# Split rows for the first two experts, and gate products put ahead of down products, in a mixture-of-experts encoder layer

## The reference, cut to what matters

```python
h = layer_norm(x) * (1 + scale2) + shift2
g = argmax over 4 groups; two best of that group's 8 experts     # hierarchical router
for each chosen expert e of a token:                               # SwiGLU, 1024 -> 512 -> 1024
    y_e = (silu(h @ w_exp_gate[e]) * (h @ w_exp_up[e])) @ w_exp_down[e]
f = sum over the two experts of weight * y_e
x = layer_norm(alpha * x + gate2 * f) * ln2_g + ln2_b
```

## Time and profile before

| | |
|---|---|
| median of 3 runs | 959.95 us (956.57 to 960.58) |
| the profiled execution | 959.74 us |
| its span, first to last instruction | 958.1 us |
| mean granted TensorE clock | 0.982 |
| PE busy | 908.5 us, 95% |
| DVE, ACT, POOL busy | 375.9, 244.6, 113.6 us |
| DMA | 295.53 MB, mean 308 GB/s |

### The profile page before, as it was taken

How to read it: one execution, slowest core, us unless ns; L and a number is a source line. 1 busy time by engine, 2 the same in 40 slices (tenths; PEclk the granted TensorE clock), 3 DMA queues, 4 the chain that set the end, 5 groups by cost and what they waited for, 6 DMA issues and landing times.

```text
span 958.1 us, 11740 instructions
## 1 busy us (share of the span) xinstructions
PE 908.5 (95%) x4381; PEld 547.7 (57%) x4381; DVE 375.9 (39%) x646; ACT 244.6 (26%) x357; POOL 113.6 (12%) x142
## 2 busy tenths in 40 slices
PE   3999999999999999999999999999998999998994
PEld 2567766888888888786454444444444444443331
DVE  4533443565344236798531232222221231322135
ACT  2422244432333225446411111101011110111024
POOL 2210366000001000000000000000000000000031
PEclk9999999999999999999999999999998999999997
DMA  9985654265565623809999999999999999999974
GB/s 370 348 282 175 253 218 177 89 230 208 200 240 147 183 91 114 278 0 401 384 404 400 410 427 425 427 424 429 429 426 424 375 395 427 426 426 427 423 290 136
DMA packets 47510, 295.53 MB, mean 308 GB/s; under 512 B 5046, under 2 KB 7190, under 8 KB 32082
## 3 DMA queue, kind: packets, MB, share of 16 engines
q1 hardware_dynamic: 37216, 263.99, 68.6%
q0 software_dynamic: 9616, 29.02, 9.0%
q10 hardware_dynamic: 610, 1.66, 0.5%
HBM read 275.81 MB, written 23.09 MB: 312 GB/s over the span
## 4 chain that ended last, share of the span: by engine, by line
PE 88%; DVE 3%; DMA 2%; issue 2%; SPq 2%; ACT 2%; POOL 0%; DVEq 0%; POOLq 0%; ACTq 0%
PE bank L627 85%; PE bank L929 2%; SPq L397 2%; DMA modraw<-in_w_mod 1%; DMA y_first<-round_y,pos_y 1%; PE bank L832 0%; PE bank L692 0%; DVE wo_lo L1766 0%; DMA round_y<-yout,store_row 0%; PE bank L911 0%; DVE y_second L2189 0%; DVE y_second L2202 0%; ACT w_hi L1181 0%; POOL y_second L615 0%; ACT sg_hid L1415 0%
## 5 line engine op out<-in xcount | busy, mean ns | idle before, releaser
L627 PE MATMUL bank<-down_w,hid_t 128*64 128x512 f32 x512 | 123.9, 627 | 8.1 <-issue 5.6
L627 PE MATMUL bank<-h_hi,w_hi 128*128 128x512 f32 x320 | 124.8, 390 | 0.3 <-ACT h_hi L1215 0.3
L627 PE MATMUL bank<-h_hi,w_lo 128*128 128x512 f32 x320 | 124.7, 390 | 0.0
L627 PE MATMUL bank<-h_lo,w_hi 128*128 128x512 f32 x320 | 124.6, 397 | 0.0
L627 PE MATMUL bank<-gate_w,x_by_pair 128*64 128x512 f32 x256 | 112.5, 592 | 0.8 <-ACT x_by_pair L1181 0.8
L627 PE MATMUL bank<-up_w,x_by_expert 128*64 128x512 f32 x256 | 112.6, 592 | 0.0
L627 PE MATMUL bank<-gate_w,x_by_expert 128*64 128x512 f32 x256 | 112.5, 592 | 0.0
L627 PE MATMUL bank<-up_w,x_by_pair 128*64 128x512 f32 x256 | 112.5, 592 | 0.0
L1415 ACT ACTIVATE sg_hid<-bank 64x512 f32<-64x512 f32 x33 | 19.5, 591 | 315.0 <-PE bank L627 315.0
L2047 DVE TENSOR_TENSOR sg_hid<-bank,sg_hid 64x512 f32<-64x512 f32 x32 | 22.2, 695 | 196.4 <-ACT sg_hid L1415 196.3
L1601 DVE TENSOR_TENSOR w_lo<-raw,w_hi 128x1024 fp32r<-128x1024 f32 x56 | 68.5, 1225 | 76.9 <-ACT w_hi L1181 76.8
(11 more groups left out here) (329 smaller groups left out, 1310.3 us busy)
## 6 DMA issues: line engine op xcount, KB each, us to landing
down_w<-in_w_exp_down SPq DMA_DIRECT2D x32, 2048.0 KB, 16.6
gate_w<-in_w_exp_gate SPq DMA_DIRECT2D x30, 2048.0 KB, 16.0
up_w<-in_w_exp_up SPq DMA_DIRECT2D x30, 2048.0 KB, 20.5
modraw<-in_w_mod SPq DMA_DIRECT2D x24, 1024.0 KB, 7.7
raw<-in_w_in SPq DMA_DIRECT2D x9, 2048.0 KB, 9.8
round_y<-zrow POOLq DMA_DIRECT2D x6, 2048.0 KB, 7.7
raw<-in_w_branch_b SPq DMA_DIRECT2D x2, 2048.0 KB, 9.5
raw<-in_w_branch_a SPq DMA_DIRECT2D x2, 2048.0 KB, 10.6
```

The lines of the kernel that those rows point to most:

```text
L627: return pe.matmul(out, lhsT, rhs, start=start, stop=stop, skip_group_check=True)
```

## The change

1. **Split rows for experts 0 and 1.** `selected_alone` is gone. The high parts are made by ScalarE in the routing stage (`high_part`), the low parts by POOL (`pool_h2lo`) instead of VectorE, each tile as soon as its high part is there. `sel` holds experts 0 and 1 from the start, and one pair of selections gives both experts' rows.
2. **Back-to-back gate products.** TensorE's order is now: gate product 0 (its second set of transposed columns comes after chunk 1), gate product 1 with the transposes of expert 0 in its middle, down product 0, selection for 2 and 3, transposes 1, down product 1. Expert 1 writes its gate product to bank 2 and its hidden rows to `sg_second`. The scaling of the residual stands behind the first silu.
3. **Loads.** Expert 3 comes in four halves instead of eight quarters, and gate/up 4 is issued ahead of down 2.
4. **The tail.** For experts 29 and 30 (`overlapped`) the gate product runs ahead of `rest(e - 1)`, and the transposes of e-1 stand in its middle.

The turns for more than 64 tokens, the semaphore counts and the buffers of the hidden rows are adapted. The core of the diff:

```diff
@@ SP
+            for half, freed, loaded in ((slice(0, KC // 2), gum_half, e_half), (slice(KC // 2, KC), m_sem["gum"], e_gu[0])):
...
+                for tile, w in ((gate_w[0], w_exp_gate), (up_w[0], w_exp_up)):
+                    sp.dma_start(tile[:, half, :], gate_src(w, 3)[:, half, :]).then_inc(loaded, 16)
+            next_gate_up(4, 1)
+            next_down(2, 0)
+            next_down(3, 1)
+            for e in range(5, NEXP - 2):
+                next_gate_up(e, e % 3)
                 next_down(e - 1, (e - 1) % 2)
@@ POOL
+            for i in range(TILES):
+                pool.wait_ge(act_h2hi, i + 1)
+                pool.wait_ge(pe_rt, 2 * i + 2)
+                pool.tensor_tensor(h2_lo[i][:, :, :], h2[i][:, :, :], h2_hi[i][:, :, :].bitcast(f32), ALU.subtract).then_inc(pool_h2lo, 1)
@@ TensorE
-            for h in range(2):
-                selected_alone(0, B[2 + h], slice(2 * h, 2 * h + 2)).then_inc(m_sem["xs"], 1)
-            for h in range(2):
-                pe.wait_ge(m_sem["xr"], h + 1)
-                x_transposes(x_rows, B[4 - 2 * h], range(2 * h, 2 * h + 2)).then_inc(m_sem["xtr"], 1)
+            selected(sel, B[2], 0, parted_rows=pool_h2lo).then_inc(m_sem["xs"], 1)
+            selected(sel, B[3], 1, range(2))
+            pe.wait_ge(act_rt, 2 * TILES + 1)
+            first_columns(0)
+            selected(sel, B[3], 1, range(2, TILES)).then_inc(m_sem["xs"], 1)
...
+            def first_experts():
+                main_gate_up(0)
+                main_gate_up(1)
+                main_down(0)
+                pe.wait_ge(dve_rt, 2)
+                turns_in_place(0)
+                pe.wait_ge(m_sem["sl"], 2)
+                selected(sel, B[4], 0).then_inc(m_sem["xs"], 1)
+                selected(sel, B[0], 1).then_inc(m_sem["xs"], 1)
+                main_transposes(1)
+                pe.wait_ge(m_sem["xr"], 3)
+                x_transposes(x_rows, B[2]).then_inc(m_sem["xtr"], 1)
+                main_down(1)
+                turns_in_place(1)
...
-                if e > 2:
+                if e > 2 and not overlapped(e):
                     rest(e - 1)
                 main_gate_up(e)
                 joined_again(pe, f"pe_{e}")
+                if overlapped(e):
+                    rest(e - 1)
@@ ScalarE
+            def high_part(i):
+                act.wait_ge(act_h2, i + 1)
+                copy(h2_hi[i][:, :, :], h2[i][:, :, :]).then_inc(act_h2hi, 1)
+
             chunk_order(2)
+            act.wait_ge(pe_out, 2 * TILES)
+            high_part(0)
             h2_columns(3, 0, (B[4], B[5]))
             chunk_order(3)
+            for i in range(1, TILES):
+                high_part(i)
...
+                main_silu(0)
+                copy(res[:, :, :], res[:, :, :], scale=ALPHA).then_inc(act_res, 1)
+                hid_columns(m_sem, B[3], hid_t, 0)
+                main_silu(1)
@@ VectorE
-            for a in range(2):
-                chosen_rows(sel[:, :, a, :], a).then_inc(m_sem["sl"], 1)
+            chosen_pair(sel, slot_of[:, 0:2, :]).then_inc(m_sem["sl"], 1)
```

More of the change, by code:

```diff
@@ L594, in expert @@
                 more, first = turns_of(e)
-                if e >= 2:
+                if e >= 2 and not overlapped(e):
                     further_rounds(e, more, first)
+                if overlapped(e + 1):
+                    further_rounds(e + 1, *turns_of(e + 1))
                 pool.wait_ge(m_sem["yo"], e + 1)
@@ L891, in _, with selected @@
             x.then_inc(pe_lg, 1)
[L893 to L903 removed]
+            def selected(chosen, bank, c, tiles=range(TILES), parted_rows=None):
+                for i in tiles:
+                    if parted_rows is not None:
+                        pe.wait_ge(parted_rows, i + 1)
                     for piece in (h2_hi, h2_lo):
@@ L1094, in with_further @@
                 more, first = turns_of(e)
-                pairs = pairs_selected(e - 1) if e > 2 else ()
+                behind = e > 2 and not overlapped(e)
+                pairs = pairs_selected(e - 1) if behind else ()
                 further_selected(first, dve_selx, e)
-                if e > 2:
+                if behind:
                     main_transposes(e - 1)
@@ L1459, in with_further @@
                 further_rows(first)
-                if e > 2:
+                if e > 2 and not overlapped(e):
                     columns_ended(e - 1)
-                gate_silu(x_sem, B[4], sg_hid, first, 1)
+                gate_silu(x_sem, B[4], further_hid_of(e), first, 1)
                 hid_columns(x_sem, B[7], hid_t_x, first)
@@ L2129, in first_experts @@
                         further_round(e, dve.snap(first + r))
+            def first_experts():
+                dve.wait_ge(m_sem["xs"], 2)
+                chosen_pair(sel, slot_of[:, 2:4, :]).then_inc(m_sem["sl"], 1)
+                hidden(0)
+                dve.wait_ge(dve_rt, 2)
+                dve.wait_ge(act_rt, 2 * TILES + 1)
+                ch.sync()
+                sides(0)
+                gate_rows(0)
+                hidden(1)
+                out_rows(0)
+                turns_in_place(0)
+                dve.tensor_scalar(next_slots[:, :], slots[:, :], float(CAP), None, ALU.add).then_inc(dve_selx, 1)
+                dve.wait_ge(m_sem["yo"], 1)
+                gate_rows(1)
+                for half, bank in enumerate((B[2], B[4])):
+                    dve.wait_ge(m_sem["xtr"], 3 + half)
+                    columns_in(x_by_expert[:, 2:4, 4 * half:4 * half + 4, :], bank).then_inc(m_sem["xt"], 1)
+                dve.wait_ge(m_sem["htr"], 2)
+                chosen_group(4)
+                out_rows(1)
+                turns_in_place(1)
             def expert(e):
```

235 lines of the change are left out of this document (98 added, 137 removed).

## The result

The changed kernel takes **966.23 us** (median of 4 runs, 965.96 to 967.61) against 960.27 for the kernel before (956.57 to 961.23), ratio 1.008 with a 95% interval of 1.0062 to 1.0099. The two medians are 6.0 us apart, by the ratio it would be 7.7: the change costs 6 to 8 us. The forecast was 959.2, the range 954.5 to 964.0, the chance of slower 0.13. The profiled execution has a span of 964.7 us against 958.1, so 6.6 us can be looked for in the two traces.

A forecast was written before the change was run, and what follows sets the result against it. The weight stream was taken to bound the kernel up to down product 18, then mostly TensorE until expert 28. Profiled 959.74 - 4.0 (start) + 3.3 (tail) = 959.0, for the median 959.2; range 954.5 to 964.0.

The forecast's parts named there:

- The split on POOL: Start: POOL's low-part subtractions slow beside DVE by 1.5 us in 7, so PE waits about 1.2 us before its selection.
- Rival (d): Start: DVE doubles POOL's last three subtractions, gate product 0 starts after about 457.5, some 5 us of stream lost; 967, chance 0.12.
- PE's own work: Start: one selection of 3.6 us and one set of four transposes of 0.62 go, 4.2 us less for TensorE.
- The stream: Start: weights land earlier through fewer, larger loads and earlier issue; gain 4.0 us by expert 5's down load, bounds 1.3 and 6.0.
- The quarters: Start: expert 3's gate and up loads in eight quarters took 11.6 us for what takes 10.1; four halves gain 1.3.
- What bounds the middle: Middle: the weight stream, 15.2 us an expert against PE's 13.4, bounds up to down product 18, shown by a 2.14 us wait.
- The tail: Last experts: PE idles 7.8 us for gate load 30; order +0.8, slow clock +2.5, together +3.3 us, bounds +0.8 and +4.8.
- d31: Tail: expert 31's down load, issued at about 912 after down product 29, still lands before its use at 928.
- The sum: Whole kernel: profiled 959.74 - 4.0 at the start + 3.3 in the tail = 959.0; 959.2 for the median.
- (a): Tail: costs only 0.8, as the clock comes back before gate product 30 or never falls; 956.8, chance 0.17.
- (b): Start: early loads don't move the stream and only the quarters count; 962.0, chance 0.13.
- (c): Start and tail: PE time counts in both, as gate load 30 lands before PE asks; 949, chance 0.08.

The follow-up runs named there:

- after_low_late: Changed kernel with POOL's low parts of tiles 1 to 3 held back until DVE has made the selection matrix; 966.18 us, ratio 1.008.
- before_pool_two: Kernel before plus three idle two-input POOL subtractions of 128x1024 where the changed kernel has its last three; 965.48 us, ratio 1.0072.
- after_low_bare: Changed kernel with POOL subtracting only 1/8 of each tile and selections using the high part twice; 958.92 us, ratio 1.0001.
- after_no_tail: Changed kernel with the old tail, no gate product ahead of a down product; 964.76 us, ratio 1.006.
- after_low_dve: Changed kernel with low parts of tiles 1 to 3 made on DVE behind the selection matrix, PE taking all high parts first; 960.68 us, ratio 1.0022.
- after_low_dve_no_tail: after_low_dve without the tail's change, both gate products behind the down products again; 958.06 us, ratio 0.9992.
- before_tail29: Kernel before with only gate product 29 put ahead of down product 28, loads in their old order; 955.99 us, ratio 0.9978.
- after_low_dve_tail29: after_low_dve with only gate product 29 ahead of its down product, loads in their old order; 956.66 us, ratio 0.998.
- before_tail_g30: Kernel before with the new tail, and gate and up load 30 issued ahead of down load 29; 955.97 us, ratio 0.9979.

## Why the prediction was wrong, point by point

- **The split on POOL: the step that failed.** I read the pair of rows 1.22 us (DVE) and 2.08 us (POOL) as "POOL slows beside DVE, DVE doesn't". The rows show one thing more: DVE had started 0.09 us earlier. Whoever starts first finishes, the other waits. At 444 us POOL starts first with instructions of 2.32 us, and the ones that wait are DVE's short ones, on the path. I took "DVE's instructions are short" as an argument against a collision; it is the worst case for one, as each of three instructions under 0.3 us waits out one of POOL's. I put 1.5 us on POOL and 0 on DVE; measured were 0 and 6.1. The Trainium skill says this outright in "SBUF — State Buffer", Who interferes with whom: the shared ports are an exclusive lock for the whole instruction and "Issue order, not op shape, decides who blocks." I had cited only the sentence of the Trainium skill's "GPSIMD Engine Reference", which says no more than that the two collide. The trace agrees for POOL's two-input instruction and for the reduction that passed, also for the tensor_scalar of `after_low_late` that took 2.20 us; for POOL's one-input instruction it does not: DVE was let in after 1.1 of 2.76 us (three of three), and there the measurement decides. A second term I had put at nothing is the clock behind the wait that this makes: about 0.9 us of selection in the changed kernel, 2.2 in `before_pool_two`.
- **Rival (d)** had the right place and the right time (967, with 0.12), by the wrong engine: it doubled POOL's subtractions. Its point of decision, gate product 0 after 457.5, held (462.6).
- **PE's own work**, 4.2 us less: right in kind, 0.8 too much. In `after_low_bare` gate product 0 starts at 455.4, 1 us earlier than forecast with 1.2 us of wait, and from there to gate product 2 it is 28.1 us where it was 31.5, 3.4 less. The two errors cancel: gate product 2 starts at 483.5, forecast 483.7. That is luck.
- **The stream**, 4.0 us by d5 (bounds 1.3 to 6.0): right, 4.0 at d5 and 3.7 at d16 and down product 17 in `after_low_bare`. (The quarters' 11.6 - 10.1 is 1.5, not the 1.3 in the sum; and no run separates the two sources.) In the changed kernel it was -2.3 and -4.6.
- **What bounds the middle: misread.** I took the wait of 2.14 us and the 16 instructions at 728.44 for down product 18. They are the selection of expert 19's second turn (`sel_x` in the row above); the last wait for weights there is down product 17 at 711.99. "15.2 us an expert" came out near enough (15.1 by d5 to d17), but the price of 6.18 - 3.65 = 2.5 us for the clock was taken from instructions of another kind. It came out right by luck, as a selection of 16 such products happens to take 3.63 us at full clock (at 462.13 in the kernel before).
- **The tail, +3.3** (bounds +0.8 to +4.8): order +0.8 forecast, 0.7 measured; clock +2.5, measured 3.2 (in one pair of profiles); idle 7.8 forecast, 7.4 measured. By the ratios the tail costs 1.9 us (after against `after_no_tail`) to 2.9 (`after_low_dve` against its kernel without the tail). The intervals of the first pair overlap, so the 1.9 is rough. Right in mechanism and size. d31, at 923.3, was in time.
- **A term I had not.** In all kernels with the new start but the last the final gathers take 8.6 to 9.05 us against 7.92, 0.7 to 1.1 us more (6.0 to 6.1 in the three that win, whose row stores take 4.9 to 5.9 in place of 2.9). I don't know why; no run isolates it.
- **The sum.** -4.0 + 3.3 describes `after_low_bare`, at 958.92 against 959.2. With the routing stopped, the start's -4.0 becomes +5.7 in the timed runs. Rivals (a), (b), (c) did not come about.

What stays open: why the stream's gain of 2 us in `after_low_dve_no_tail` is only 0.5 us in the time (0.9992, interval to 1.0005). The profile points to waits and clock in the tail, which is argued from one execution.

## What to carry to other kernels

Before work is moved to POOL, look at what DVE runs in that stretch: not how busy it is but whether a chain of short two-input instructions on the path lies there; each can wait out one whole two-input POOL instruction that has started before it. And to the price of a wait of TensorE add the slow clock that may follow it: 2.2 us behind a wait of 4.5 here, nothing behind one of 2.2. Where weights stream through a queue that never empties, lay the landing times of the last loads beside the order in which TensorE asks for them before reordering either: the same two gate products lose 0.3% or win 0.2% by which load is issued first. And name the tile of an instruction group before taking a wait in front of it as evidence for a bound.

## What the hardware showed that I had not expected

- A POOL subtraction of 128x1024 with two inputs (1.86 to 2.32 us) keeps a DVE instruction of 0.17 to 0.28 us waiting for up to 2.2 us and is not slowed itself. One with a single input (2.76 us) lets DVE in 1.07 to 1.10 us after its own start.
- Small POOL instructions are dear: 128x1024 in eighths took 3.6 us a tile (10.81 for three), against 2.32 whole.
- After the wait of 7.4 us the granted clock stayed at 0.50 for another 5 us of full work (901 to 906). For short waits the length alone doesn't tell: 1.9 us in `before_tail29` and 2.4 in `after_low_dve_tail29` left it at 1.00, the same 1.9 us in `before_tail_g30` (0.66 in the mean of 5 us) and 1.67 us in front of down product 17 of the kernel before (0.68) didn't.
